# Attention of a transformer block: value product from halves in three passes, with its operands' remainders made on three engines

## The reference

```python
s = (jnp.einsum('bqhd,bkhd->bhqk', qn, k_nope)
     + jnp.einsum('bqhr,bkr->bhqk', qr, k_rope)).astype(jnp.float32) * sm_scale
s = jnp.where(allowed[None, None], s, NEG_INF)      # blocks of 64 tokens, causal
p = jax.nn.softmax(s, axis=-1).astype(v.dtype)
return jnp.einsum('bhqk,bkhd->bqhd', p, v)
```

## Time and profile before

| what | value |
|---|---|
| median of 3 runs | 2050.96 us (2047.62 to 2051.68) |
| profiled execution | 2051.85 us, span 2050.1 us, mean granted TensorE clock 0.952 |
| TensorE busy | 1856.4 us, 91% of the span |
| VectorE, ScalarE, GpSimd busy | 1221.2, 724.0, 499.6 us |
| attention | from about 444 us to 1109 us of the span |

### The profile page before, as it was taken

One profiled execution on the slowest core, in us unless ns is written; L12 is line 12 of the kernel. 1 busy time (PEld: TensorE's weight loads), 2 busy tenths in 40 slices (PEclk: granted clock), 3 DMA queues, 4 the chain that ended last, 5 costly groups with the idle time before them and its releaser, 6 DMA issues. The chain is left out here.

```text
span 2050.1 us, 27268 instructions
## 1 busy us (share of the span) xinstructions
PE 1856.4 (91%) x8737; PEld 1440.7 (70%) x8738; DVE 1221.2 (60%) x2097; ACT 724.0 (35%) x1205; POOL 499.6 (24%) x550
## 2 busy tenths in 40 slices
PE   2999999997999999999996999983999999999970
PEld 2677878764666666666664788872899999999960
DVE  5688889856675675675674655546344444444444
ACT  2545354325444444444444323320222222222214
POOL 0131414112211221221221111103234343434330
PEclk9999999997999999999998899985999999999995
DMA  7655656520000000000002444424799999999958
GB/s 274 197 176 159 197 144 170 149 62 1 8 9 6 8 8 6 8 8 5 8 8 97 168 144 143 157 80 154 232 274 273 277 269 277 268 279 269 278 100 328
DMA packets 216128, 290.79 MB, mean 142 GB/s; under 512 B 24341, under 2 KB 172016, under 8 KB 215802
## 3 DMA queue, kind: packets, MB, share of 16 engines
q1 hardware_dynamic: 193466, 220.60, 32.5%
q0 software_dynamic: 20224, 69.22, 13.7%
q10 hardware_dynamic: 2368, 0.17, 0.1%
HBM read 229.13 MB, written 60.82 MB: 141 GB/s over the span
## 5 line engine op out<-in xcount | busy, mean ns | idle before, releaser
L901 PE MATMUL tbank<-probs,VV 128*128 128x512 f32 (+3 forms) x640 | 293.0, 539 | 1.3 <-ACT probs L1119 1.2
L983 DVE TENSOR_REDUCE cmax<-tbank 128x1 f32<-128x512 f32 (+2 forms) x340 | 205.8, 606 | 98.9 <-PE tbank L826 92.7
L1119 ACT ACTIVATE probs<-tbank 128x512 f32<-128x512 f32 (+1 forms) x320 | 169.7, 533 | 234.2 <-PE tbank L872 230.1
L381 PE MATMUL pbank<-hhi,wslhi 128*128 128x512 f32 x512 | 206.8, 404 | 7.4 <-DVE wsllo L432 6.7
L870 PE MATMUL tbank<-Qhi,Khi 97*128 97x512 f32 (+2 forms) x321 | 212.5, 662 | 0.0
L1877 DVE TENSOR_SCALAR xTe<-ebank,modcol 128x256 f32<-128x256 f32 (+1 forms) x128 | 53.7, 472 | 258.6 <-PE ebank L1795 137.2
L1145 POOL TENSOR_SCALAR diag<-cst,nmax 128x128 fp32r<-128x128 f32 x138 | 84.4, 612 | 485.7 <-DVE nmax L986 485.4
L381 PE MATMUL pbank<-hhi,wsllo 128*128 128x512 f32 x512 | 201.2, 393 | 0.0
L381 PE MATMUL pbank<-hlo,wslhi 128*128 128x512 f32 x512 | 200.9, 392 | 0.0
L1817 PE MATMUL ebank<-xTe,wg 128*128 128x192 f32 x1024 | 171.8, 326 | 3.1 <-DVE ahi L1905 1.8
L1817 PEld LDWEIGHTS ebank<-xTe,wg 128*128 128x128 f32 x1024 | 167.9, 190 | 7.9 <-DVE ahi L1905 2.1
(11 more groups left out here) (273 smaller groups left out, 3488.6 us busy)
## 6 DMA issues: line engine op xcount, KB each, us to landing
wg<-in_w_exp_gate SPq DMA_DIRECT2D x32, 1024.0 KB, 6.1
wu<-in_w_exp_up SPq DMA_DIRECT2D x32, 1024.0 KB, 9.5
wd<-in_w_exp_down SPq DMA_DIRECT2D x32, 1024.0 KB, 7.6
wraw<-in_w_in SPq DMA_DIRECT2D x60, 512.0 KB, 4.2
wmod<-in_w_ada POOLq DMA_DIRECT2D x64, 256.0 KB, 3.5
wada<-in_w_ada SPq DMA_DIRECT2D x2, 4096.0 KB, 21.0
xt<-in_x SPq DMA_DIRECT2D x4, 2048.0 KB, 12.3
mixed<-mix_dram SPq DMA_DIRECT2D x16, 512.0 KB, 4.4
```

Of the source, the lines that this page charges most:

```text
L381: ins = pe.matmul(out, w[:, S % 3, k], h[:, n % 2, k], start=k == 0 and j == 0, stop=k == KD - 1 and j == 2)
L901: ins = pe.matmul(out, VV[:, kt, 2 * b:2 * b + 2].rearrange("p c d -> p (c d)"), step_of(probs, m), start=kt == 0, stop=last)
L983: W(ve.tensor_reduce(cmax[:, i % 2, n:n + 1], plain[:, chunk % 2, 0:w], AX.X, ALU.max), plain_read)
L1119: A(act.activation(step_of(probs, m), scores[:, m % 2, j * P:512], ACT.Exp), exp_done)
```

## The change

The value product is taken from halves. Values are kept as a rounded float32r part `VVhi` and a remainder `VVlo`, probabilities as `phi` and `plo`. `value(m)` becomes two float32r passes (`VVhi` by `phi`, `VVlo` by `phi`), and a third one, `VVhi` by `plo`, comes `LAG` = 2 steps later (`value_low`). To have the parts:

- ScalarE takes each exponential twice, once rounded into `phi`, once in full into `probs` (which now lies in the space of `KR`); GpSimd subtracts the two into `plo` (`prob_low`). All three are rings of 4 steps; ScalarE waits for the remainder of four steps before;
- VectorE subtracts the rounded values from the made ones in PSUM (`lower_values`);
- ScalarE instead of GpSimd fills the columns of ones (and of zeros for the remainder), and zeros for the two corrections that the first head's first steps take from a head that isn't there.

The product of turned queries goes back into PSUM, and the add reads it from there. `copy_out` is done in two steps of a group (kt = 2 and 3), two pieces each. ScalarE's loop over pairs is written out four times instead of a hardware loop. Parts 1 to 7 come a step later, values parts two or three steps later, and so do the divisions by one or two. The clearing of an output bank by VectorE goes (a product does it), and ScalarE waits for the second key remainder (`rope_rest`) before its loop.

```diff
-PART_AT = {2 + 3 * c: c for c in range(8)}
+PART_AT = {2 + 3 * c + (c > 0): c for c in range(8)}
...
 V_PARTS = NT // 4
-V_AT = [(1, STEPS_HEAD - NT + 4 * (v + 1)) if v < V_PARTS - 1 else (0, 1) for v in range(V_PARTS)]
+LAG = 2
+RING = 4
+V_AT = [(1, STEPS_HEAD - NT + 4 * (v + 1) + LAG) if v < V_PARTS - 1 else (0, LAG + 2) for v in range(V_PARTS)]
 V_EARLY = V_PARTS - 1
...
-DIVIDE_AT = {m: (g, r) for g, steps in ((GROUPS - 1, (6, 7)), (0, (12, 13)), (1, (18, 19)), (2, (28, 29)))
+V_EARLY_BANK = (0, 1, 4)
+DIVIDE_AT = {m: (g, r) for g, steps in ((GROUPS - 1, (7, 8)), (0, (13, 14)), (1, (19, 20)), (2, (30, 31)))
              for r, m in enumerate(steps)}
...
-        VV = sb("VV", [P, NT, 4, VD])
-        probs = sb("probs", [P, 4 * 512])
-        qf, turned_q = sb("qf", [P, 2, 512]), sb("turned_q", [P, 512])
+        VVhi, VVlo = sb("VVhi", [P, NT, 4, VD], F32R), sb("VVlo", [P, NT, 4, VD], F32R)
+        phi, plo = sb("phi", [P, RING, 512], F32R), sb("plo", [P, RING, 512], F32R)
+        probs = KR[:].rearrange("p (r n) -> p r n", r=RING)
+        qf = sb("qf", [P, 2, 512])
...
             for v in range(V_EARLY):
-                pe.wait_ge(made_dve, V_EARLY_AFTER[v])
+                if v < 2:
+                    pe.wait_ge(made_dve, v + 1)
+                else:
+                    pe.wait_ge(qf_ready, 1)
                 make_values(v, 0, bank[:, V_EARLY_BANK[v]])
-            pe.wait_ge(made_dve, 6)
+            pe.wait_ge(made_dve, 4)
...
-            pe.wait_ge(filled, 2)
-            pe.wait_ge(v_copied, V_EARLY)
+            pe.wait_ge(filled, 7)
+            pe.wait_ge(v_lowered, V_EARLY)
...
+            def heads_values(v, kt, b):
+                return v[:, kt, 2 * b:2 * b + 2].rearrange("p c d -> p (c d)")
+            def value_low(m, b, first):
+                g, kt = STEP_OF[m]
+                last = kt == GQ * (g + 1) - 1
+                pe.wait_ge(plo_done, first + (m + 1 + RING))
+                ins = pe.matmul(outp[:, g % 2, first_tile(g, kt) * P:512], heads_values(VVhi, kt, b),
+                                step_of(plo, m), start=False, stop=last)
+                if last:
+                    ins.then_inc(out_done, 1)
+            pe.matmul(outp[:, 1].rearrange("p (a n) -> p a n", n=VD), onesr[:], VVhi[:, 0:512 // VD, 1], start=True, stop=False)
...
-                        pe.wait_ge(exp_done, hp * 2 * STEPS_HEAD + (b * STEPS_HEAD + m + 1))
+                        pe.wait_ge(phi_done, hp * 2 * STEPS_HEAD + (b * STEPS_HEAD + m + 1))
...
                         if b == 0 and m == 0:
-                            pe.wait_ge(v_copied, hp * V_PARTS + V_EARLY)
+                            pe.wait_ge(v_lowered, hp * V_PARTS + V_EARLY)
                         if b == 0 and (g, kt) == (GROUPS - 1, 4 * V_EARLY):
-                            pe.wait_ge(v_copied, hp * V_PARTS + V_PARTS)
-                        j = first_tile(g, kt)
-                        out = outp[:, g % 2, j * P:512]
-                        last = kt == GQ * (g + 1) - 1
-                        ins = pe.matmul(out, VV[:, kt, 2 * b:2 * b + 2].rearrange("p c d -> p (c d)"),
-                                        step_of(probs, m), start=kt == 0, stop=last)
-                        if last:
-                            ins.then_inc(out_done, 1)
+                            pe.wait_ge(v_lowered, hp * V_PARTS + V_PARTS)
+                        out = outp[:, g % 2, first_tile(g, kt) * P:512]
+                        pe.matmul(out, heads_values(VVhi, kt, b), step_of(phi, m), start=kt == 0, stop=False)
+                        pe.matmul(out, heads_values(VVlo, kt, b), step_of(phi, m), start=False, stop=False)
...
+                            if b == 0 and c == 1:
+                                pe.wait_ge(v_lowered, hp * V_PARTS + V_PARTS)
                             if c == 0:
...
-                                    pe.wait_ge(v_copied, hp * V_PARTS + V_PARTS)
+                                    pe.wait_ge(v_lowered, hp * V_PARTS + V_EARLY)
                                 else:
-                                    pe.wait_ge(made_dve, nxt * 8)
+                                    pe.wait_ge(qf_ready, nxt * 4)
+                            elif c % 2:
+                                pe.wait_ge(made_dve, nxt * 4 + (c + 1) // 2)
                             else:
-                                pe.wait_ge(made_dve, nxt * 8 + c)
+                                pe.wait_ge(qf_ready, nxt * 4 + c // 2)
                             make(c, 1 - b)
...
                         if (b, m) in V_AT:
                             v = V_AT.index((b, m))
                             if v == 0:
-                                pe.wait_ge(made_dve, nxt * 8 + 8)
+                                pe.wait_ge(qf_ready, nxt * 4 + 4)
+                            elif v == V_PARTS - 1:
+                                pe.wait_ge(made_dve, nxt * 4 + 1)
                             else:
-                                pe.wait_ge(v_copied, hp * V_PARTS + (v if b == 0 else V_PARTS + v))
+                                pe.wait_ge(v_lowered, hp * V_PARTS + (V_PARTS + v))
                             make_values(v, hp + b)
                         value(m)
+                        if m >= LAG:
+                            value_low(m - LAG, b, hp * 2 * STEPS_HEAD + b * STEPS_HEAD)
+                        else:
+                            value_low(m - LAG + STEPS_HEAD, 1 - b, hp * 2 * STEPS_HEAD + (b - 1) * STEPS_HEAD)
...
+            for m in range(STEPS_HEAD - LAG, STEPS_HEAD):
+                value_low(m, 1, (HEADS - 1) * STEPS_HEAD)
...
                     W(ve.tensor_tensor(qf[0:QKD, n % 2], made[0:QKD], cs[0:QKD, at], ALU.mult))
-                    W(ve.tensor_tensor(turned_q[NOPE:QKD], made[QKD:P], cs[QKD:P, at], ALU.mult), made_dve)
                     W.wait()
-                    W(ve.tensor_tensor(qf[NOPE:QKD, n % 2], qf[NOPE:QKD, n % 2], turned_q[NOPE:QKD], ALU.add),
-                      qf_ready)
+                    W(ve.tensor_tensor(made[NOPE:QKD], made[QKD:P], cs[QKD:P, at], ALU.mult))
+                    W.wait()
+                    W(ve.tensor_tensor(qf[NOPE:QKD, n % 2], qf[NOPE:QKD, n % 2], made[NOPE:QKD], ALU.add), qf_ready)
...
+            def lower_values(v, pair, src=made):
+                ve.wait_ge(v_copied, pair * V_PARTS + (v + 1))
+                at = slice(v * 4, (v + 1) * 4)
+                W(ve.tensor_tensor(VVlo[:, at, 0::2], src.rearrange("p (t c d) -> p t c d", c=2, d=VD),
+                                   VVhi[:, at, 0::2].bitcast(F32), ALU.subtract), v_lowered)
...
+                if 0 < n <= V_EARLY:
+                    lower_values(n - 1, 0, bank[:, V_EARLY_BANK[n - 1]])
...
-            W(ve.memset(outp[:, 1], 1.0), out_set)
...
+                        if (b, m - 1) in V_AT:
+                            lower_values(V_AT.index((b, m - 1)), hp + b)
...
-            def copy_out(g, head):
-                act.wait_ge(out_done, head * GROUPS + (g + 2))
-                act.wait_ge(divided, head * GROUPS + (g + 2))
-                for h in range(2):
-                    half = slice(h * VD, (h + 1) * VD)
-                    act.activation(raw[half, g % 2, 0], outp[0:VD, g % 2, h * 256:(h + 1) * 256], ACT.Copy)
-                    ins = act.activation(raw[half, g % 2, 1], outp[VD:P, g % 2, h * 256:(h + 1) * 256], ACT.Copy)
-                A(ins, out_free)
+            def copy_out(h, g, head):
+                if h == 0:
+                    act.wait_ge(out_done, head * GROUPS + (g + 2))
+                    act.wait_ge(divided, head * GROUPS + (g + 2))
+                half = slice(h * VD, (h + 1) * VD)
+                act.activation(raw[half, g % 2, 0], outp[0:VD, g % 2, h * 256:(h + 1) * 256], ACT.Copy)
+                ins = act.activation(raw[half, g % 2, 1], outp[VD:P, g % 2, h * 256:(h + 1) * 256], ACT.Copy)
+                if h == 1:
+                    A(ins, out_free)
...
+                v, k = (VVhi, VVlo)[n % 2], n // 2 * 2 + 1
+                A(act.activation(v[:, :, k], cst[:, C_ONE:C_ONE + VD].unsqueeze(1).to_broadcast([P, NT, VD]), ACT.Copy,
+                                 scale=1.0 - n % 2), filled)
+            for k in (0, 2):
+                A(act.activation(VVhi[:, NT - LAG:, k], cst[:, C_ONE:C_ONE + VD].unsqueeze(1).to_broadcast([P, LAG, VD]),
+                                 ACT.Copy, scale=0.0), filled)
+            A(act.activation(plo[:, RING - LAG:].rearrange("p r (a n) -> p (r a) n", n=P),
+                             cst[:, C_ONE:C_ONE + P].unsqueeze(1).to_broadcast([P, LAG * 4, P]), ACT.Copy, scale=0.0), filled)
...
-            act.wait_ge(out_set, 1)
-            with act.Fori(0, HEADS // 2) as hp:
+            act.wait_ge(rope_rest, 2)
+            for hp in range(HEADS // 2):
                 for b in range(2):
                     for m in range(STEPS_HEAD):
                         g, kt = STEP_OF[m]
                         j = first_tile(g, kt)
```

(54 more changed lines are left out.)

## The result

| | before | after |
|---|---|---|
| median of 4 runs, same chip | 2050.64 us | 2063.18 us (2058.82 to 2066.42) |
| ratio, 95% interval | | 1.0049 [1.0034, 1.0065] |
| profiled execution, span, clock | 2051.85, 2050.1, 0.952 | 2058.82, 2057.0, 0.947 |

The prediction was 2030 us, a gain; the change costs time instead: 12.5 us by the medians, 10 by the ratio (7 to 13 by its interval).

A forecast was written before the change was run, and what follows sets the result against it. TensorE was taken to set the pace in the attention stage. The value product's -37.3 us and the smaller terms summed to -21.1, from 2051.85 to 2030.8, scaled to 2030 us; the range ran from 2010 to 2058.

The forecast's parts named there:

- Value product: On TensorE, three float32r passes instead of one float32 product save 4.66 us a head: -37.3 us in 8 heads.
- ScalarE's bunch: Copy-out, query split and maxima copy on top of the exponential pairs at steps 26 and 27 outrun the cushion: +5.6 us.
- Copy-out: Four copy-out pieces in a row at a group's first step go, and with them some TensorE waits: -2.4 us.
- GpSimd: In-order remainders and diagonals from step 25 to 36 run the cushion out in four b=0 heads: +2 us.
- rival 3: GpSimd becomes the bound through its order, idling 1.28 us at each of 16 diagonals a head: 2075 us; chance 0.12.
- Weight copies: VectorE's copies before a head's first key product may collide with a GpSimd subtraction: +3 us.
- rival 2: GpSimd's subtractions lock out VectorE's weight copies too, TensorE waiting each head: 2057 us, 2043 with half hit; chance 0.11.
- Loop turns: TensorE, arriving sooner, waits longer for weights at VectorE's loop turns, less the table load's knock-on: +0.8 us.
- ScalarE's written-out pairs: ScalarE's table load (1.28 us, judged hidden) goes in three of four loop turns; its knock-on saves 3 x 0.3 us.
- Start: Before the loop, a value remainder and the wait for the key remainder delay the first exponential: +3.9 us.
- Moved value part: A value part made at step 4 instead of 1 in b=0 heads waits for the first key remainder: +2.8 us.
- the end: Two short correction products at the kernel's end wait for GpSimd: +0.5 us.

The follow-up runs named there:

- e7: Changed kernel with the divisions of group 2 at steps 32 and 33 instead of 30 and 31: 2032.93 us, ratio 0.9905 to the kernel before.
- e1: Changed kernel with the divisions of group 2 at steps 37 and 38 instead of 30 and 31: 2032.35 us, ratio 0.991 to the kernel before.
- e2: Changed kernel with the division's product replaced by a reciprocal with one SBUF input, output not divided: 2043.28 us, ratio 0.9955 to the kernel before.
- e9: e10 with the turned queries kept in SBUF, so their add has two SBUF inputs again: 2030.23 us, ratio 0.9901 to the kernel before.
- e10: e5 with TensorE's loop over pairs written out too: 2020.31 us, ratio 0.9843 to the kernel before.
- e14: e10 with both halves of the sums copied out in one step (kt = 2): 2027.2 us, ratio 0.9887 to the kernel before.
- e5: e1 with VectorE's loop over pairs written out: 2022.19 us, ratio 0.9866 to the kernel before.
- e8: e5 with ScalarE's loop over pairs as a hardware loop again: 2040.06 us, ratio 0.9936 to the kernel before.
- e6: Kernel before, plus a GpSimd subtraction of two SBUF tiles in each step, result unread: 2068.32 us, ratio 1.0076 to the kernel before.

## Why the prediction was wrong

**The step that failed** is in VectorE's part: "the divisions stay, 4 a head, with slack behind them". I had the row of the collision and took its 1.0 us as the price of one, because beside the one subtraction it could last no longer. The same paragraph put GpSimd at four fifths of the time. A product that isn't let in between one such subtraction and the next is then held to the end of their row, and that row ends where GpSimd waits for a maximum, which VectorE makes after the product. The slack was there (1.55 to 2.17 us) and was enough for 1.0, and for e7's 2.11, but not for 3.35 and 4.91. Priced at nothing, it took 18.2 us, and with the low clock some 30. Without it, as e1 has it, the kernel takes 2032 us where 2030 was forecast.

The Trainium skill (SBUF — State Buffer, section Who interferes with whom), which I used, has the exclusion for an instruction's whole length; the runs agree for two inputs (e2 against the kernel after, e9 against e10), and one copy beside a subtraction agrees too (1.34 us for 0.26). The trace shows in addition that the product that waits may stay out through several of GpSimd's instructions (4.91 us), though in eight places it got in between two.

The other terms, by what the runs measured:

- **Value product, -37.3:** right in kind and nearly in size. The full step is 1.63 us, and TensorE's busy time is 33.5 us less in e10's heads. Where the other tenth went is open.
- **ScalarE's bunch, +5.6:** mis-sized. TensorE waits 0.21 us a head at step 27 or 28, 1.7 us in all. But the cushion is thin: with the copies in one step (e14) it is 7 us more.
- **Copy-out, -2.4:** hardly there to be saved. Before, the value products themselves waited for an exponential only at the loop's start (1.2 us). The weight loads' waits, from which I took the term, grew from 20.8 to 26.7 us, nearly all under running products: the products waited 2.7.
- **GpSimd, +2, and rival 3:** no product waits for a remainder, in any head. GpSimd has 116.9 us a pair where 118 was predicted, and a backlog, as I had argued against the rival. That very backlog is what made the lock long.
- **Weight copies, +3, and rival 2:** one copy of 36 is long (1.34 us, at 490.22, beside the first subtraction), the rest 0.17 to 0.28. They follow the maximum that GpSimd's next diagonal needs too, so beside them run that diagonal (570.61 to 571.28 beside the copies from 570.50 to 571.14) and at most the last 0.1 us of a subtraction. The rival's mechanism exists; its collisions hardly occur. (By its own terms the rival with half the copies hit comes to 2042, not 2043.)
- **Loop turns, +0.8:** far too small, 10 us by e5. I counted the added wait for the weights only. At the turn the maxima are late too (1.54 to 1.64 us, where before it was 0.28 at one turn), presumably since TensorE now comes sooner, and the clock falls.
- **ScalarE's written-out pairs, 0.9 saved:** worth 18 us beside a doubled exponential (e8). I judged the table load hidden by the trace of before, where ScalarE had half the work.
- **Start, +3.9:** the first exponential moves from 486.30 to 488.90, +2.6. The table load (1.28 us) now lies under the wait for the key remainder, where I had put it behind.
- **Moved value part, +2.8:** TensorE waits for the first key remainder four times, 1.9 us in all.
- **The clock:** absent from my sum. Every stall was priced at its own length, and 18.2 us of stalls brought 12 us more.

Gains that were too large (value product by 4, copy-out by 2) and turns that were too small (by 9) stand against costs that were too large (bunch, copies, GpSimd, start, moved part: 11 together). They nearly cancel, which is luck, and e1 lands on the forecast. That 2032 is near 2030 thus proves only the large terms. I gave the slower side 0.13, nearly all of it on rival 3, the wrong engine.

**What stays open:** the clock after a stall. It fell after five of the eight stalls (as low as 0.50) and stayed at 1.00 after the other three, one of them (at 715.74) as long as the first, and so the three pairs are 154.7, 157.4 and 159.0 long. Which idle time brings it down was not settled. The moved value part was read from the trace alone, and the end (+0.5) was not tested.

## What to carry to other kernels

When an engine gets much new SBUF work, list every instruction on the engine it shares SBUF with that reads two SBUF inputs, and price each by the distance to the other's next pause as the worst case, not by one instruction; if that pause hangs on work queued behind the victim, as here, the price was the longest in the trace. Then move it to where a pause follows, or let it read PSUM. And once TensorE is close to full, price a stall at more than its length (here 18.2 us of stalls cost 30), and loop turns on the other engines again.

## What the hardware did that I had not expected

- A 0.43 us product took 4.91 us beside five GpSimd instructions back to back; in four kernels such a product ended 0.28 to 0.30 us after GpSimd's last subtraction did.
- With one input from SBUF, 33 instructions of 1753 ns varied by 3 ns in the same surroundings.
- 1.5 to 2.7 us of idle time in a full stream was in most cases (8 of 11) followed by some microseconds at 0.50 granted, in which each 512-column pass starts 0.43 us after the last instead of 0.23. In e6, with stalls of up to 1.26 us, the loop's clock stayed at 1.00.
- A turn of a hardware loop is 3.14 us without issue on VectorE, and on ScalarE 2.17 us and a table load of 1.28. Written out on TensorE and GpSimd, the loop made no difference that could be measured (2022.19, 2020.31 and 2020.91 us).
- VectorE's copies of 0.17 to 0.28 us beside GpSimd's diagonal kept their length; the diagonals there took 0.66 to 0.73 us where the median is 0.60. A product that starts 0.08 us before a subtraction (step 20 of each head) takes its 0.43 us.
